# Two transformer blocks on one core: block products from the seventh pair on, and another order in the second output projection

## The reference

```python
def swiglu(x, w_in, w_out):
    gate, up = jnp.split(x @ w_in, 2, axis=-1)
    return (jax.nn.silu(gate) * up) @ w_out

def second_block(...):
    h = h + 0.5 * swiglu(rmsnorm(h, ffn1_norm[l]), ffn1_w_in[l], ffn1_w_out[l])
    h = h + hybrid_mixer(rmsnorm(h, mix_norm[l]), ...)     # ends in o @ w_mix_out
    h = h + 0.5 * swiglu(rmsnorm(h, ffn2_norm[l]), ffn2_w_in[l], ffn2_w_out[l])
```

## Time and profile before

| | us |
|---|---|
| median of three runs | 1612.99 |
| lowest, highest | 1612.87, 1613.27 |
| the profiled execution's own time | 1612.32 |
| its span | 1610.5 |
| PE busy in it | 1589.0 |
| DVE, ACT, POOL busy | 966.2, 761.2, 886.7 |
| block products of instance 1 on PE | 712.00 to 866.59 |
| block products of instance 2 on PE | 1324.20 to 1478.8 |

### The profile page before, as it was taken

One profiled execution on the slowest core, in us unless ns is written; L12 is line 12 of the kernel. 1 busy time (PEld: TensorE's weight loads), 2 busy tenths in 40 slices (PEclk: granted clock), 3 DMA queues, 4 the chain that ended last, 5 costly groups with the idle time before them and its releaser, 6 DMA issues.

```text
span 1610.5 us, 23966 instructions
## 1 busy us (share of the span) xinstructions
PE 1589.0 (99%) x9196; PEld 1351.1 (84%) x9196; DVE 966.2 (60%) x1592; ACT 761.2 (47%) x1391; POOL 886.7 (55%) x641
## 2 busy tenths in 40 slices
PE   9999999999999999999999999999999999999997
PEld 8787878888888888889998887877767889999886
DVE  7176756884444225878884434576783587886224
ACT  6366655543344324545554323577573445555222
POOL 7424354575445553558889553654114548889650
PEclk9999999999999999999999999999999999999999
DMA  5411103322323222323333222322012323233221
GB/s 209 151 53 53 40 14 105 117 93 93 104 92 104 93 95 76 105 93 105 105 106 105 93 95 74 120 93 80 27 28 92 99 98 105 96 103 106 96 100 53
DMA packets 49682, 147.56 MB, mean 92 GB/s; under 512 B 5152, under 2 KB 13728, under 8 KB 49568
## 3 DMA queue, kind: packets, MB, share of 16 engines
q1 hardware_dynamic: 48232, 143.39, 26.8%
q10 hardware_dynamic: 1336, 2.63, 0.5%
HBM read 142.84 MB, written 3.41 MB: 91 GB/s over the span
## 4 chain that ended last, share of the span: by engine, by line
PE 81%; DVE 2%; POOL 1%; ACT 1%; issue 1%; DMA 1%; SPq 0%; DVEq 0%; ACTq 0%
PE PS L621 14%; PE PS L623 14%; PE PS L622 14%; PE PS L2154 7%; PE PS L2155 6%; PE PS L2156 6%; PE PS L1413 4%; PE PS L582 4%; PE PS L1424 3%; PE PS L590 2%; PE PS L1074 2%; PE PS L1096 2%; PE PS L1121 1%; POOL w_lo L683 1%; DMA stage<-in_weights 1%
## 5 line engine op out<-in xcount | busy, mean ns | idle before, releaser
L683 POOL TENSOR_TENSOR w_lo<-stage,w_hi 128x512 fp32r<-128x512 f32 x402 | 567.3, 1438 | 598.6 <-ACT w_hi L657 597.7
L657 ACT ACTIVATE w_hi<-stage 128x1024 fp32r<-128x1024 f32 x262 | 270.5, 1054 | 303.3 <-DMA stage<-in_weights 289.4
L621 PE MATMUL PS<-H_hi,w_hi 128*128 128x512 f32 x512 | 199.4, 389 | 0.4 <-DVE rcol L1622 0.4
L622 PE MATMUL PS<-H_lo,w_hi 128*128 128x512 f32 x512 | 199.3, 389 | 0.0
L623 PE MATMUL PS<-H_hi,w_lo 128*128 128x512 f32 x512 | 199.2, 389 | 0.0
L621 PE MATMUL PS<-A_hi,w_hi 128*128 128x512 f32 x496 | 193.2, 389 | 0.6 <-DVE A_lo L829 0.6
L623 PE MATMUL PS<-A_hi,w_lo 128*128 128x512 f32 x496 | 193.0, 389 | 0.0
L622 PE MATMUL PS<-A_lo,w_hi 128*128 128x512 f32 x496 | 193.0, 389 | 0.0
L2128 POOL TENSOR_TENSOR S_lo<-S_f,S_hi 128x512 fp32r<-128x512 f32 x90 | 126.5, 1421 | 66.5 <-DVE S_f L1988 37.7
L2128 POOL TENSOR_TENSOR w_lo<-stage,w_hi 128x512 fp32r<-128x512 f32 x90 | 141.8, 1603 | 0.0
L2154 PE MATMUL PS<-F,w_hi 128*128 128x256 f32 x480 | 137.5, 287 | 1.7 <-ACT conv L2047 1.1
(11 more groups left out here) (295 smaller groups left out, 3583.2 us busy)
## 6 DMA issues: line engine op xcount, KB each, us to landing
stage<-in_weights SPq DMA_DIRECT2D x254, 512.0 KB, 3.4
stage<-in_weights SPq DMA_DIRECT2D x32, 128.0 KB, 2.8
out_t<-Y SPq DMA_DIRECT2D x8, 256.0 KB, 2.0
X<-in_x_t SPq DMA_DIRECT2D x3, 512.0 KB, 8.4
bias_line<-bias_line ACTq DMA_DIRECT2D x1, 1270.0 KB
strip<-bias_line ACTq DMA_DIRECT2D x1, 1024.0 KB, 5.0
stage<-in_weights SPq DMA_DIRECT2D x2, 256.0 KB, 4.1
V<-QF SPq DMA_DIRECT2D x4, 128.0 KB, 2.7
```

What stands on the lines that cost most here:

```text
L621: pe.matmul(out, a, h_hi, start=first, stop=False, skip_group_check=skip)
L622: pe.matmul(out, a, h_lo, start=False, stop=False, skip_group_check=skip)
L657: act.activation(w_hi[:, slot, :], stage[:, slot, :], ACT.Copy).then_inc(hi_done, 1)
L683: lo = pool.tensor_tensor(w_lo[:, slot, cols], stage[:, slot, cols], w_hi[:, slot, cols].bitcast(F32), ALU.subtract)
```

## The change

Four things change. (1) `PLAIN` goes from 7 to 6, so pair 6 of instances 1 and 2 becomes a block pair, and the banks, the form order and the copies' places follow. (2) The preparation is spread anew: the corner and the sums of the first block pair come after pair 4, before the last low parts; PE waits for each form by itself where it waited for all seven; in the first block pair ACT makes the u3 copy ahead of the next pair's `S_hi`. (3) In the last pair the second half of product 4 is run after product 5. (4) In the second output projection bank 7 comes first and bank 6 second, the wait for the last use of bank 6 moves to the second output, and of the early outputs three take their last two groups right after output 4's six groups.

```diff
-PLAIN = 7
+PLAIN = 6
...
-WO_ORDER2 = [6, 7, 0, 1, 2, 3, 4, 5]
+WO_ORDER2 = [7, 6, 0, 1, 2, 3, 4, 5]
...
                 elif inst and n == 4:
-                    dve_forms_lo(dve, inst, range(3, 7))
-                elif inst and n == 5:
                     dve_corner_lo(dve, inst, u_up, PLAIN)
                     for k in range(4):
                         dve_sum(dve, inst, u_up, PLAIN, k)
+                    dve_forms_lo(dve, inst, range(3, 5))
+                elif inst and n == 5:
+                    dve_forms_lo(dve, inst, range(5, 6))
...
-            pe.wait_ge(qk_evac[1], len(EVAC2))
             pe.wait_ge(cm["used"], TB)
             for at in range(3):
+                if at == 1:
+                    pe.wait_ge(qk_evac[1], len(EVAC2))
...
                 run(pe_wo1(pe, b, at, range(6)))
                 if b == 0:
                     run(pe_turn1(pe, at + 3))
-            for g in (6, 7):
+                else:
+                    for early in {3: (0, 1, 2), 4: (3, 4)}[at]:
+                        run(pe_wo1(pe, b, early, (6, 7)))
+            for g in (6, 7) if b == 0 else ():
...
+        FORMED = [8, 9, 11, 8, 10, 12, 8]
...
-                fast.formed.wait(act, inst, 8 if k < 3 else 12)
+                fast.formed.wait(act, inst, FORMED[k])
...
                 act_keep(act, inst, n, "u2")
+                if n == PLAIN:
+                    act_keep(act, inst, n, "u3")
                 if more:
                     act_sum_half(act, inst, n + 1, 0)
                     act_sum_half(act, inst, n + 1, 1)
-                act_keep(act, inst, n, "u3")
+                if n > PLAIN:
+                    act_keep(act, inst, n, "u3")
...
                 if more:
                     dve_corner_lo(dve, inst, u_up, n + 1)
+                    if n == PLAIN:
+                        dve_forms_lo(dve, inst, range(6, 7))
                     dve_sum(dve, inst, u_up, n + 1, 0)
...
-            fast.form_lo.wait(pe, inst, 7)
+            form_ready(PLAIN, 0)
...
-                product_of(corner("a", n), *unit_half(ug, 1), 1, True).then_inc(unit_done, 1)
+                form_ready(n, 3)
+                last = n + 1 == FC
+                p2 = product_of(corner("a", n), *unit_half(ug, 1), 3, True, range(2 if last else 4))
+                if not last:
+                    p2.then_inc(unit_done, 1)
...
+                if last:
+                    product_of(corner("a", n), *unit_half(ug, 1), 3, False, range(2, 4)).then_inc(unit_done, 1)
```

More of the change, by code:

```diff
@@ L1912, in build @@
         T1_HI, T1_LO, T2_HI, T2_LO, T3_HI, T3_LO = range(6)
-        FORMS = [(F1, B11_HI, B11_LO), (F1, B21_HI, B21_LO), (F1, B22_HI, B22_LO), (F2, T1_HI, T1_LO),
-                 (F2, T2_HI, T2_LO), (F2, T3_HI, T3_LO), (F1, T4_HI, T4_LO)]
+        FORMS = [(F1, B11_HI, B11_LO), (F2, T1_HI, T1_LO), (F2, T2_HI, T2_LO), (F1, B21_HI, B21_LO),
+                 (F2, T3_HI, T3_LO), (F1, T4_HI, T4_LO), (F1, B22_HI, B22_LO)]
+        FORMED = [8, 9, 11, 8, 10, 12, 8]
         def form_f(k):
@@ L1932, in dve_form_sums @@
         def dve_form_sums(dve, inst):
-            b11, b21, b22, t1, t2, t3, t4 = [form_f(k) for k in range(7)]
+            b11, t1, t2, b21, t3, t4, b22 = [form_f(k) for k in range(7)]
             b12 = F1_f[:, B12_F, :, :]
@@ L2147, in pe_fast, with product_of @@
         def pe_fast(pe, inst, u_up):
-            def product_of(bank, hi, lo, form, first):
+            def product_of(bank, hi, lo, form, first, ks=range(4)):
                 where, h, l = FORMS[form]
-                for k in range(4):
+                for k in ks:
                     cols = bass.ts(k, P)
@@ L2179, in p1, with form_ready @@
                 product_of(corner("b", n), w_hi[:, ug % RING, 0:T], A11_lo[:, :], 0, True).then_inc(fast.spent.sem, 1)
-            fast.form_lo.wait(pe, inst, 7)
+            def form_ready(n, form):
+                if n == PLAIN:
+                    fast.form_lo.wait(pe, inst, form + 1)
+            form_ready(PLAIN, 0)
             p1(PLAIN)
@@ L2187, in pe_fast @@
                 bank_free("c", n, 4)
-                product_of(corner("c", n), *sum_parts(n, 0), 3, True).then_inc(fast.spent.sem, 1)
+                form_ready(n, 1)
+                product_of(corner("c", n), *sum_parts(n, 0), 1, True).then_inc(fast.spent.sem, 1)
                 fast.sum_lo.wait(pe, inst, q + 2)
                 fast.snapped.wait(pe, inst, q + 1)
-                product_of(corner("b", n), *sum_parts(n, 1), 4, False).then_inc(fast.spent.sem, 1)
+                form_ready(n, 2)
+                product_of(corner("b", n), *sum_parts(n, 1), 2, False).then_inc(fast.spent.sem, 1)
                 pe.wait_ge(lo_done, ug + 1)
                 bank_free("a", n, 1)
-                product_of(corner("a", n), *unit_half(ug, 1), 1, True).then_inc(unit_done, 1)
+                form_ready(n, 3)
[3 more added lines that the diff above has]
+                    p2.then_inc(unit_done, 1)
                 fast.sum_lo.wait(pe, inst, q + 3)
                 fast.snapped.wait(pe, inst, q + 2)
-                product_of(corner("b", n), *sum_parts(n, 2), 5, False).then_inc(fast.spent.sem, 1)
+                form_ready(n, 4)
+                product_of(corner("b", n), *sum_parts(n, 2), 4, False).then_inc(fast.spent.sem, 1)
+                if last:
+                    product_of(corner("a", n), *unit_half(ug, 1), 3, False, range(2, 4)).then_inc(unit_done, 1)
                 if n + 1 < FC:
@@ L2201, in pe_fast @@
                 fast.snapped.wait(pe, inst, q + 3)
-                product_of(corner("b", n), *unit_half(uv, 1), 6, False).then_inc(fast.spent.sem, 1)
+                form_ready(n, 5)
+                product_of(corner("b", n), *unit_half(uv, 1), 5, False).then_inc(fast.spent.sem, 1)
                 fast.block.wait(pe, inst, 4 * (n - PLAIN) + 2)
-                product_of(corner("c", n), *unit_half(uv, 0), 2, False).then_inc(unit_done, 1)
+                form_ready(n, 6)
+                product_of(corner("c", n), *unit_half(uv, 0), 6, False).then_inc(unit_done, 1)
         @block.sync
```

## The result

The changed kernel takes 1615.24 us (20 runs, 1614.62 to 1615.55), the kernel before 1612.91 (20 runs beside them, 1612.6 to 1613.53). The ratio is 1.0014, with a 95% interval of 1.0007 to 1.002: 2.3 us slower, where +1.4 was forecast. The profiled execution took 1615.37 us, its span is 1613.6.

The account below looks back on a forecast made before the run. PE, busy 1589.0 of 1610.5 us, was taken to bound the kernel. Instance 1 +2.3, instance 2 +0.5 and projection -1.45 gave +1.4 us on 1612.32, or 1614.4 after 0.67 for the median; range over the cases 1609.6 to 1616.9.

Parts of the forecast that it names:

- The block pair: Pair 6 as block pair: saves 0.80 us per instance, but waits and hitches outweigh it in both instances.
- Product 6 of pair 6: PE waits for the u3 copy, held by pair 5's gate product: +1.81 us in instance 1, none in instance 2.
- the timetable: Worked order of the four queues around the first block pair; instance 1's gate of pair 5 ends at 711.05.
- Product 4 of pair 7: PE waits for POOL's rest of the gate unit: +1.12 us in instance 1, +1.05 in instance 2.
- The hitches: PE's 0.25 us delay before product 6, now in pairs 7 to 20: +0.9 us in each instance.
- The rival in which the start is never made good: Block pairs: wait stays or hitch doubles, 28 pairs cost 0.25 us more each: +7, 1621.4 us; chance 0.09.
- The split: Pair 21: half of product 4 run after product 5 covers the u3 copy, -0.75 us in each instance.
- The projection: Second output projection: waits for output 7 and bank 6 shrink, -1.04 - 0.41 = -1.45 us.
- The wait for bank 6: Second projection, at 1190.98: 0.59 us and 0.11 restart go, but DVE's pace limits the gain to -0.41 us.
- output 7: Second projection: its wait for POOL's rest goes since the slot frees 6.8 us sooner, -1.04 us.
- the start of the up projection: After the second projection: 0.3 us of wait on POOL stays.
- DVE keeps its lead: Rival: start waits of 2.93 and 1.19 us vanish, 1610.3 us, or 1608.5 with free pairs; chance 0.24.

Follow-up runs that it names:

- experiment 2: Changed kernel with the first block pair's u3 copy in a place of its own, not waiting for pair 5's gate product: 1614.86 us, ratio 1.0012.
- the cut corner: Changed kernel with the corner of pairs 8 to 21 made on 64 of its 512 columns: 1607.87 us, ratio 0.9969.
- the value half in PSUM: Changed kernel with DVE's first value half of block pairs but the last kept in PSUM, to relieve the port shared with POOL: 1608.23 us, ratio 0.9969.
- the kernel with both gains: Kernel before with the split product 4 in the last pair and the new second-projection order, seven plain pairs kept: 1609.83 us, ratio 0.9982.
- experiment 3: Kernel before with split and new projection, DVE's first read on 16 of 256 columns from the third block pair on: 1609.90 us, ratio 0.9981.

## Why the prediction was right, and where it was off

The direction, the size class and most steps came out. The forecast was 1614.4, the result 1615.2, inside the range.

- **The block pair: right in kind, 1 us too small.** The prediction's +4.3 for the pair without split (its terms of +3.05 and +1.25) measured +5.3 alone.
- **Product 6 of pair 6, the term that was mis-sized.** Worked +1.81 and 0.14, measured 2.20 (2.12 and 0.08 at the restart) and 0.48. The gate product began 0.98 later than in the timetable, at 711.43 for 710.45, while PE had come only 0.80 later to the stretch (701.93 for 701.13). That is 0.18 of DVE. The copy began 0.77 after the gate product's start where the timetable has 0.64, another 0.13. That leaves 0.08 of the 0.39 open. In instance 2 the miss is 0.34, of the same size.
- **The cause of that wait was put too narrowly.** The prediction said that product 6 wants the u3 copy, and that the gate product holds it. The gate product did hold it, but experiment 2 shows that nothing hung on it: with the copy freed PE waited 1.9 us at product 7. The late party is DVE's queue with POOL in its way, and each of its steps there is just the one that PE meets first.
- **Product 4 of pair 7.** Worked +1.12 and +1.05, measured 1.05 and 1.07 (0.95 and 0.10; 0.97 and 0.10).
- **The hitches.** One in each of pairs 7 to 20, as said: 0.29 us in pair 7 and 0.17 to 0.21 after it, each with 0.07 at the restart. The forecast +0.9 rested on 0.25 each. In all they are 3.8 us an instance, where the trace before has 2.6 and 2.7, so +1.2 and +1.1: this term too was 0.2 to 0.3 too small in each instance. The rival in which the start is never made good fell with it: no pair after 7 waits at product 4.
- **The split.** -0.75 for each instance was worked; alone it measured -1.45 in all by the medians, and 0.59 and 0.64 in the stretches of its trace, where two starts in pair 21 are still late by 0.07. Where the other 0.2 lies is not shown. DVE was not late at product 7.
- **The projection.** Worked -1.45, measured -1.7 alone and -1.66 between the landmarks. The sum fits, but two of its terms were off and cancelled, which was luck. The wait for bank 6 is gone, worked as -0.41, yet the stretch from the matmuls ahead of it (1187.29 before, 1190.92 after) to output 4's groups (1214.58 and 1218.10) is only 0.11 shorter: a wait of 0.29 for ACT's `O` is new, and the matmul behind it starts 0.45 late. From there to the first matmul of the up projection (1247.40 and 1249.51) it is 1.41 shorter. 1.04 of that is output 7, as worked; 0.30 is the start of the up projection, of which the prediction said that its wait stays: the last projection matmul and the first of the up projection were 0.53 apart before, and are 0.23 apart after.
- **DVE keeps its lead, the rival with 0.24**, fell in all runs with six plain pairs, with the port relieved too.

The errors partly cancelled: the pair's +1.0 against -0.2 of the projection. With product 6 and the hitches at their measured sizes the sums of the two block stretches would be +2.9 and +1.1, where +2.82 and +1.06 were measured.

## What to carry to other kernels

Ask of a wait whether it is the cause or only the first place where a late queue is met. If the queue is late, freeing one consumer moves the wait to the next one, and the sum stays. A faster form of the main work is worth its difference only while the preparing engines keep up. Look at the exchange between these engines before their busy time: 0.18 us a pair off the rhythm of DVE and POOL was worth 5.2 us here, because PE no longer met them, and 0.25 us of DVE work outside it nothing.

## What the runs showed of the hardware

**After stands of 2 to 3 us PE's granted clock was halved in four traces and not in two others.** The changed kernel without projection and split stands 2.12 us at product 6, as the changed kernel does. Its busy times and granted clock in the stretches during and after it (columns as in the earlier trace rows):

```profile
710.00:712.16 2.16, 0.20 (x2) 0.03 (x1) 2.16 (x5) 0.48 (x2) 0.00 (x0) 1.00 0.04 15
712.16:714.90 2.74, 2.74 (x14) 2.74 (x15) 2.47 (x6) 2.34 (x6) 1.55 (x2) 0.57 0.04 9
714.90:718.50 3.60, 3.60 (x28) 3.60 (x27) 2.06 (x3) 2.12 (x3) 3.60 (x4) 0.85 0.20 35
```

Sixteen matmuls of 128x256 start 0.21 instead of 0.12 apart, the lower of the two levels, 1.2 GHz: 1.4 us. The same follows the stands of 2.12 us with the cut corner, 2.04 with the value half in PSUM and six plain pairs, and 3.2 with the u3 copy back in its old place. In the changed kernel's trace the clock stayed at 1.00 behind a stand of 2.12 us, and so it did behind 2.03 us at product 7 in experiment 2; what decides is not shown. Here it cost little: PE then met product 4 of pair 7 without the wait of 0.95, and pair 7 had no hitch. Instance 1 took 169.09 us, against 168.29 of the changed kernel plus the 0.75 of the missing split. Most of the slow clock fell into time in which PE would have waited for the same queues. Over many executions it seems not quite free: 11 of the changed kernel's 20 have a mean granted clock of 0.997, and take 1615.30 us in the mean where the other nine take 1615.04; with the value half in PSUM as well, five at 0.997 take 1608.34 and two at 0.999 take 1607.76. That the stand is what lowered their mean clock is likely, as the profiled execution of the latter had 0.997, but those executions have no trace.

**A narrow step can take as long as a wide one.** On 64 columns the corner still took 881 ns in the mean, beside POOL, where 512 columns took 917 in the kernel with both gains. Its own work can be little of that, since a step on 16 columns took 161 ns in experiment 3 (a read of PSUM, beside POOL as well). The gain shows on POOL and in DVE's later steps: the second sum on DVE takes 0.68 us in pair 14, where it takes 1.78 in the changed kernel. The row is of the kernel with the cut corner:

```profile
L2010 DVE TENSOR_TENSOR A_lo<-stage,w_hi 128x64 fp32r<-128x64 f32 x8 | 7.0, 881 | 0.0
```
